# Down projection of a hybrid decoder step with seven products per pair of output tiles, and a new order around its compressed attention

## What is computed

```python
def conformer_conv(u, buf, w, b, ln_g, ln_b):          # width 31, each channel by itself
    xx = jnp.concatenate([buf, u], 1)
    y = dwconv_valid(xx, w) + b
    return jax.nn.silu(layer_norm(y, ln_g, ln_b)), xx[:, -(CONV_WIDTH - 1):]

def conv_ffn(h, buf, w_up, cw, cb, w_down):
    z = h @ w_up
    gate, up = z[..., :D_FF], z[..., D_FF:]
    gc = dwconv_valid(jnp.concatenate([buf, gate], 1), cw) + cb
    return (jax.nn.silu(gc) * up) @ w_down, ...
...
x = x + jnp.concatenate([o_nsa, c], -1) @ w_out
x = x + conv_ffn(rms_norm(x, ffn_g), ...)              # D_FF = 2816, D_MODEL = 1024
```

## Time and profile before

| | |
|---|---|
| median of 3 runs | 2145.61 us (2143.18 to 2148.26) |
| the profiled execution's own time | 2146.83 us |
| its span, first to last instruction | 2145.0 us |
| granted TensorE clock, mean | 0.959 of full |
| TensorE busy with matmuls | 2032.3 us, 95% |
| TensorE weight loads (beside them) | 1567.8 us, 73% |
| VectorE busy | 1154.1 us, 54% |
| ScalarE busy | 365.6 us, 17% |
| GpSimd busy | 113.5 us, 5% |
| DMA queues, share of 16 engines | 23.6% and 4.0% |
| chain that ended last | PE 90%, DVE 6%, ACT 3%, issue 1% |

### The profile page before, as it was taken

One profiled execution on the slowest core, in us unless ns is written; L12 is line 12 of the kernel. 1 busy time (PEld: TensorE's weight loads), 2 busy tenths in 40 slices (PEclk: granted clock), 3 DMA queues, 4 the chain that ended last, 5 costly groups with the idle time before them and its releaser, 6 DMA issues.

```text
span 2145.0 us, 26339 instructions
## 1 busy us (share of the span) xinstructions
PE 2032.3 (95%) x9926; PEld 1567.8 (73%) x9926; DVE 1154.1 (54%) x2762; ACT 365.6 (17%) x957; POOL 113.5 (5%) x219
## 2 busy tenths in 40 slices
PE   8999779999999999999999988799989999999999
PEld 5767656777777777777776677567767777777777
DVE  4997566554066666600069974755431767765000
ACT  1012156212110000100000121652221100000000
POOL 1002030000000000000000020300000000000000
PEclk9998679999999999999999986899999999999999
DMA  6203262652312222111231022226522122221112
...
DMA packets 109985, 200.23 MB, mean 93 GB/s; under 512 B 13698, under 2 KB 81555, under 8 KB 104611
## 3 DMA queue, kind: packets, MB, share of 16 engines
q1 hardware_dynamic: 103618, 167.01, 23.6%
...
## 4 chain that ended last, share of the span: by engine, by line
PE 90%; DVE 6%; ACT 3%; issue 1%; DMA 0%; POOL 0%; DVEq 0%
PE ps L908 26%; PE ps L536 18%; PE ps L689 9%; PE ps L549 9%; PE ps L579 8%; PE ps L977 2%; PE ps L861 2%; PE ps L735 2%; PE ps L521 2%; PE ps L807 1%; PE ps L766 1%; PE ps L674 1%; PE ps L595 1%; PE ps L752 1%; PE ps L618 1%
## 5 line engine op out<-in xcount | busy, mean ns | idle before, releaser
L536 PE MATMUL ps<-rC,rB 128*128 128x288 f32 x1056 | 257.1, 406 | 0.0
L536 PEld LDWEIGHTS ps<-rC,rB 128*128 128x128 f32 x1056 | 200.6, 190 | 55.4
L1395 DVE SCALAR_TENSOR_TENSOR catT<-XC,par,catT 128x512 f32<-128x512 f32 x240 | 180.4, 752 | 8.3
L1811 DVE TENSOR_TENSOR xT<-xT,ps 128x576 f32<-128x576 f32 x14 | 10.6, 754 | 289.2 <-PE ps L536 250.9
L908 PE MATMUL ps<-catT,rD 128*128 128x288 f32 x528 | 131.6, 406 | 0.0
L689 PE MATMUL ps<-WR,rD 128*128 128x254 f32 x512 | 120.7, 393 | 0.0
L908 PEld LDWEIGHTS ps<-catT,rD 128*128 128x128 f32 x528 | 100.3, 190 | 27.7
L908 PE MATMUL ps<-catT,XC 128*128 128x288 f32 x480 | 119.8, 406 | 0.4 <-DVE rD L1766 0.4
L908 PE MATMUL ps<-rA,WR 128*128 128x288 f32 x448 | 117.8, 406 | 0.0
L689 PEld LDWEIGHTS ps<-WR,rD 128*128 128x128 f32 x512 | 99.9, 197 | 16.6 <-issue 0.3
L908 PEld LDWEIGHTS ps<-catT,XC 128*128 128x128 f32 x480 | 91.0, 190 | 26.2 <-issue 1.2
...
## 6 DMA issues: line engine op xcount, KB each, us to landing
...
WR<-in_kvc SPq DMA_DIRECT2D x128, 128.0 KB
...
```

What stands on the lines that cost most here:

```text
L536: ins = mm(ps[:, bank + hf, 0:HN], w[:, k * P:(k + 1) * P], rhs[:, k, hf * HN:(hf + 1) * HN], start=k == 0, stop=k == K - 1)
L1395: stt(yc[:, 0:SEQ], xc[:, k:k + SEQ], w, yc[:, 0:SEQ], ALU.mult, ALU.add)
```

## The change

Four things.

**contract** makes the output tiles in four pairs q. The product of a pair of output tiles with the 22 tiles of `actT` is cut into 2 x 2 blocks both ways (two output tiles, two halves of 11 tiles (FH), left and right columns) and made with seven products of 11 `mm` each, p1 to p7, which stand for eight. Four of them read sums of weight blocks (DS1 to DS4, by `s1` to `s4`, for each pair) and four read sums of activations (DT1 to DT3, `b12` in place, DT4, by `t1` to `t4`, once a layer), all made by VectorE. VectorE adds each product to the quarters of `xT` that it belongs to, in one instruction with the bank broadcast. Two weight tiles now lie in all of `rB` (`DW[0]`), the next two in `rD` (`DW[1]`), and a pair's loads wait for the pair that had the place; the first load into `rD` also waits for the layer's `ff` output to be written. In the last pair of layer 0 the order is p1, p2, p7, p6, p4, p5, p3. As the second tile of pair 0 lies where ring slots 4 and 5 are, the last pair of expand, f = 21, goes to slots 0 and 1, which pair 19 holds. The next layer's w_qkv is loaded before its w_glu, and w_glu waits for DS1 to DS3, which lie in `WR`.

**taps** runs the taps over the prompt's tokens alone, with a `step` after each; the samples' convolution of a tile is one product of 64 x 31 elements, one sum over the 31 and one addition of the bias.

**compress**: all five `heads(t)` come ahead of `ln_var` and the reciprocal; ScalarE squares the heads of tiles 2 to 4 first (tile 4 into a place of its own in `rA`).

**compressed scores**: `keys_T` and `cmp_scores` run within `hidden(l, 1, 1)`, after 4 and 8 of its 16 `mm`; the sample's second products, the first two prompt scores and `cmp_turned` are interleaved at the start of `prompt`, and VectorE's and ScalarE's orders follow.

The diff, cut to its core (indentation shortened):

```diff
+        def up_slots(f):
+            return (0, 1) if f == FT - 1 else ((2 * f + 4) % 6, (2 * f + 5) % 6)
...
-        s = (n + 4) % 6
+        s = up_slots(n // 2)[n % 2]
         seen_of["unit_made"] += 1
         if n >= 2:
-            sp.wait_ge(sh["unit_made"], seen_of["unit_made"] - 6)
+            sp.wait_ge(sh["unit_made"], seen_of["unit_made"] - (6 if n // 2 < FT - 1 else 3 + n % 2))
...
+        if l:
+            for ch in range(2):
+                qkv(l, ch)
         for s in range(4):
+            if l and s % 2 == 0:
+                sp.wait_ge(sh["down_made"], 28 * l - (1 if s else 3))
             ring(s, I["w_glu"][l, s])
-        if l:
-            sp.wait_ge(*count("down_made", KD))
-        for ch in range(2):
-            qkv(l, ch)
-        if l:
-            sp.wait_ge(*count("ff_out", 16))
+        if l == 0:
+            for ch in range(2):
+                qkv(l, ch)
+        else:
+            sp.wait_ge(sh["down_made"], 28 * l)
         sp.dma_start(rD[:, 4096:8192], I["w1"][l]).then_inc(sh["w1_in"], 16)
...
-        sp.wait_ge(sh["unit_made"], seen_of["unit_made"])
+        sp.wait_ge(sh["unit_made"], seen_of["unit_made"] - 2)
         down(l, 1)
+        sp.wait_ge(*count("act_done", FT))
         if l + 1 < DEPTH:
-            sp.wait_ge(*count("act_done", FT))
             sp.dma_start(par[:, :], I["par"][l + 1]).then_inc(sh["par_in"], 16)
+        sp.wait_ge(*count("ff_out", 16))
         for m in range(2, KD):
-            sp.wait_ge(sh["down_made"], l * KD + m - 1)
+            if m >= 4 and m % 2 == 0:
+                sp.wait_ge(sh["down_made"], 28 * l + 7 * (m // 2 - 1))
             down(l, m)
+        sp.wait_ge(sh["down_made"], 28 * l + 21)
...
-        prompt_hidden(l, 1)
-        keys_T(NCS)
+        prompt_hidden(l, 1, lambda: keys_T(NCS))
         prompt_second(l, 0)
         hidden(l, 1, 0)
         prompt_second(l, 1)
-        keys_T(NCP)
-        cmp_scores(l)
-        hidden(l, 1, 1)
-        sample_second(l, 1, 0, CG[0])
-        sample_second(l, 1, 1, CG[0])
-        cmp_turned()
-        pe.wait_ge(sh["vct_kept"], NJOB * l + 3)
+        hidden(l, 1, 1, {3: lambda: keys_T(NCP), 7: lambda: cmp_scores(l)})
...
+        pe.wait_ge(*count("cs_max"))
         scores(0)
+        sample_second(l, 1, 0, CG[0])
+        sample_second(l, 1, 1, CG[0])
+        scores(1)
         keys_T(NCS)
-        scores(1)
+        cmp_turned()
         pe.wait_ge(sh["kct_kept"], NJOB * l + 3)
+        pe.wait_ge(sh["vct_kept"], NJOB * l + 3)
         pe.wait_ge(*count("ct_kept", 2))
...
+        def product(bank, w, h, each=None):
+            for k in range(FH):
+                if each:
+                    pe.wait_ge(*count(each))
+                ins = mm(ps[:, bank, 0:HN], w(k), h(k), start=k == 0, stop=k == FH - 1)
+            ins.then_inc(sh["down_made"], 1)
...
+            def p1():
+                after(ahead + 1)
+                product(0, lambda k: w[:, 0, k], lambda k: actT[:, k, left], None if q else "act_done")
+            def p2():
+                after(ahead + 5)
+                product(1, lambda k: w[:, 0, FH + k], lambda k: actT[:, FH + k, left], None if q else "act_done")
+            def p3():
+                after(ahead + 6, ds=4)
+                product(4, lambda k: DS4[k // 4][:, k % 4], lambda k: actT[:, FH + k, right])
+            def p4():
+                after(ahead + 7, dt=4)
+                product(5, lambda k: w[:, 1, FH + k], lambda k: DT4[k // 5][:, k % 5])
+            def p5():
+                after(ahead + 3, ds=1, dt=1)
+                product(2, lambda k: DS1[:, k], lambda k: DT1[:, k])
+            def p6():
+                after(own + 2 if q else 0, ds=3, dt=3)
+                product(1 if q else 6, lambda k: DS2[:, k], lambda k: actT[:, k, right])
+            def p7():
+                after(ahead + 4, ds=2, dt=2)
+                product(3, lambda k: DS3[k // 10][:, k % 10], lambda k: DT3[:, k])
...
+            p1()
+            if q and not last:
+                square_sum(2 * q - 2, 6, sq2, KD)
+            p2()
+            if q and not last:
+                square_sum(2 * q - 1, 6, sq2, KD)
+            if q < 3 or last:
+                p5()
+                p7()
+                p6()
+                p3()
+                p4()
+                count("x_upd", 2)
+            else:
+                p7()
+                p6()
+                p4()
+                p5()
+                half_sum(6, 6, 0, False)
+                half_sum(7, 6, 0, True)
+                p3()
+                pe.wait_ge(*count("x_left", 2))
                 pe.wait_ge(*count("x_upd"))
-            if m == 0:
-                for f in range(FT):
-                    pe.wait_ge(*count("act_done"))
-                    for hf in range(2):
-                        ins = mm(ps[:, hf, 0:HN], WD[:, 0, f * P:(f + 1) * P], actT[:, f, hf * HN:(hf + 1) * HN],
-                                 start=f == 0, stop=f == FT - 1)
-            else:
-                ins = unit(WD[:, m % 2], actT, 2 * (m % 2), FT)
-            ins.then_inc(sh["down_made"], 1)
-            if m and not last:
-                square_sum(m - 1, 6, sq2, KD)
+                half_sum(7, 6, 1, False)
+            if q == 0 and not last:
+                pe.wait_ge(sh["d_added"], 28 * l + 5)
...
+        head_squares(*TT[3])
+        head_squares(*TT[4])
...
+        turned_heads(2)
         root(lnrs)
-        head_squares(*TT[4])
-        turned_heads(2)
         tanhed(CG[0][0], NCS)
         turned_heads(3)
         tanhed(CG[0][1], NCS)
-        act.wait_ge(*count("qk_done", 2))
+        act.wait_ge(*count("qk_done", 3))
         turned_heads(4)
...
-                stt(yc[:, 0:SEQ], xc[:, k:k + SEQ], w, yc[:, 0:SEQ], ALU.mult, ALU.add)
-                ins = stt(ys, xs[:, :, k:k + DS], w, ys, ALU.mult, ALU.add)
-            if k < CW - 1:
-                step(ins)
+                ins = stt(yc[:, 0:SEQ], xc[:, k:k + SEQ], w, yc[:, 0:SEQ], ALU.mult, ALU.add)
+            step(ins)
         if last == CW:
-            ins.then_inc(sh["conv_made"], 1)
+            xs, ys = xc[:, XS0:XW], yc[:, SEQ:NT]
+            every = bass.AP(xs.tensor, xs.offset, [list(xs.ap[0]), [XSEG, DB], [1, DS], [1, CW]])
+            w = PV[:, 16 + 34 * c:16 + 34 * c + CW].unsqueeze(1).unsqueeze(1).to_broadcast([P, DB, DS, CW])
+            step(tt(TM.rearrange("p (b n k) -> p b n k", b=DB, n=DS), every, w, ALU.mult))
+            step(dve.tensor_reduce(ys, TM.rearrange("p (n k) -> p n k", k=CW), X, ALU.add))
+            ts(ys, ys, PV[:, 16 + 34 * c + CW:17 + 34 * c + CW], None, ALU.add).then_inc(sh["conv_made"], 1)
...
         head_means(1)
         heads(0)
+        heads(1)
+        head_means(2)
         ln_centre()
-        head_means(2)
-        heads(1)
-        ln_var()
         head_means(3)
         heads(2)
+        head_means(4)
+        heads(3)
+        heads(4)
+        ln_var()
+        dve.wait_ge(*count("posb_kept"))
+        gelu_in(0, NCS, 0)
         dve.wait_ge(*count("std_made"))
         step(dve.reciprocal(lnrs, lnrs))
-        head_means(4)
-        heads(3)
-        dve.wait_ge(*count("posb_kept"))
-        gelu_in(0, NCS, 0)
-        heads(4)
         gelu_in(1, NCS, 0)
...
         mask(0)
+        gelu_out(1, NCS, 0)
+        cmp_weight()
+        key_means(NCS)
+        mask(1)
+        weight(0)
         key_norm(NCS)
-        for v in range(16):
+        if l:
+            dve.wait_ge(sh["s_kept"], l * NPR)
+        dve.wait_ge(*count("tr_kept", 10))
+        for h in range(2):
+            hp = slice(HD * h, HD * (h + 1))
+            for g in range(G):
+                ins = dve.tensor_copy(QB[hp, :, 32 * h + 8 * g:32 * h + 8 * g + 8],
+                                      QT[hp, g, SEQ:NT].rearrange("p (b i) -> p b i", b=DB))
+        ins.then_inc(sh["qb_made"], 1)
+        for v in range(1, 16):
...
+        def t1():
+            tt(DT1, b12, b11, ALU.subtract).then_inc(sh["dt_made"], 1)
+        def t3():
+            tt(DT3, b22, b12, ALU.subtract).then_inc(sh["dt_made"], 1)
+        def t2():
+            dve.wait_ge(sh["dt_made"], 4 * l + 2)
+            tt(b12, b22, DT1, ALU.subtract).then_inc(sh["dt_made"], 1)
+        def t4():
+            dve.wait_ge(sh["dt_made"], 4 * l + 3)
+            for i, (a, b) in enumerate(((0, 5), (5, 10), (10, 11))):
+                ins = tt(DT4[i], b21[:, a:b], b12[:, a:b], ALU.subtract)
+            ins.then_inc(sh["dt_made"], 1)
+        def s1(q):
+            dve.wait_ge(*count("wb_in" if q % 2 else "wa_in", 32))
+            w = DW[q % 2]
+            tt(DS1, w[:, 1, 0:FH], w[:, 1, FH:FT], ALU.add).then_inc(sh["ds_made"], 1)
+        def s3(q):
+            w = DW[q % 2]
+            tt(DS3[0], w[:, 0, 0:10], w[:, 1, 0:10], ALU.subtract)
+            tt(DS3[1], w[:, 0, 10:FH], w[:, 1, 10:FH], ALU.subtract).then_inc(sh["ds_made"], 1)
+        def s2(q):
+            dve.wait_ge(sh["ds_made"], 16 * l + 4 * q + 2)
```

(65 more changed lines are left out.)

159 lines of the change are left out of this document (86 added, 73 removed).

## The result

The changed kernel takes 2075.97 us (median of 4 runs, 2074.83 to 2076.76) and the kernel before, run beside it on the same chip, 2144.69 (2143.18 to 2148.26): a ratio of 0.9677 with a 95% interval of 0.966 to 0.9694, so 68.7 us or 3.2% faster. The forecast was 2090 and 55.3 gained, with a range of 2077 to 2103. The profiled execution of the changed kernel took 2076.76 and its span is 2075.0, against 2146.8 and 2145.0 before: 70.1 less, 14.8 more than forecast on the same footing.

What follows compares the result with a forecast made beforehand. TensorE, busy 95% of the span, was taken as the bound. Contract 42.7, less expand 15.1, plus compress 19.6, scores 7.8 and the end 0.3 gave 55.3 us gained, median 2090, range 2077 to 2103.

Steps and rivals of the forecast that it cites:

- Contract: Contract, both layers: 308 `mm` a layer in place of 352, 42.7 us gained, VectorE's sums costed at nothing.
- Expand: Expand's last ring slot: pair 21 loads later, TensorE waits 5.85 a layer, plus 1.7 of clock; 15.1 lost together.
- one fall costs 1.6, and I add 1.7 a layer: Expand, after the new hole: TensorE's clock falls, 1.7 us a layer added, between ends of nothing and 3.
- Taps: Taps: a tile 1.4 us better, but glu(3) and `project` 1.3 late; the end of the taps 0.4 earlier.
- Compress: Compress: heads ahead of the norm let `prompt_T` begin 9.5 us earlier, 10.1 in layer 1; sum 19.6.
- Scores within the MLP: From L635 to the third scores: two holes filled, then VectorE bounds; 3.9 us gained a layer, 7.8 in both.
- Rival (b): Clock stays up in expand's hole and through `prompt_hidden` and the MLP after: 12.2 us, time 2078; chance 0.13.
- a clock above 0.97: Sign listed as showing the prediction wrong: TensorE's granted clock above 0.97.
- (a): Contract: VectorE's sums come late, p6 waits 6.2 us a layer, 12.4 in all, time 2103; chance 0.12.
- (c): Compress and prompt: waits only change names, root and reciprocal hold TensorE; 27.4 us gone, time 2118; chance 0.07.
- (d): Taps: samples' product may pay by the row, slower than before; 2165 us at 14 a tile; chance 0.02.
- (e): Expand: the ring change costs nothing, as loads come earlier than read; time 2075 us; chance 0.02.

Runs made afterwards that it cites:

- b1_fill_heads: Changed kernel with six extra products (12 records) in the hole ahead of `prompt_T`: 2065.06 us, ratio 0.9632.
- c4_all: Changed kernel with ring change undone, two contract waits later, VectorE's taps dealt otherwise, third scores ahead of the samples' turned keys: 2041.17 us, ratio 0.9532.
- c5_all_filled: c4_all with two extra products (4 records) ahead of the prompt's transposes: 2043.03 us, ratio 0.9535.

## Why the prediction was right or wrong

The direction and the parts were right, and the sum came out 14.8 low. The steps that failed are two terms of the clock: the stretch at contract's start was not taken away (3.4), and the records whose holes were filled were costed at the old clock (4.8). The rest is 3.5 in compress, 1.6 of queue in the scores' part, 2.0 of chance at the start, less 0.5 elsewhere.

**Contract.** Right in kind: 616 records, no wait for VectorE. The term was mis-sized, 43.0 with the end for 46.2, since the working called contract "a solid line, 88 records in 21.34 us", while the row above it in the earlier trace rows had 23.27 for the first tile. Those 1.9 were a stretch at the lower clock, present in both layers before and in neither after. The step that failed is "Expand ... one fall costs 1.6, and I add 1.7 a layer": I added a fall in the new hole and did not take away the one that stood at contract's start. The two experiments on the ring and the filled hole show that it is one stretch that moves. Without the stretch contract is 1.7 a layer shorter (176 records in 42.92 and not 44.60), so by the traces the hole costs 11.8 net (15.2 less 3.4) and not 15.1; the run of it alone gave 8.5, and 12.2 in the profiled execution.

**Expand.** The hole was forecast as 5 for the load and 1 for the sums, then 1.7 of clock. It is 5.2, no wait for the sums (8 records at the lower clock, 4.18, cover VectorE's 2.7), and 2.5 of clock: 7.7 and 7.5 against 7.55. The sum agreed, with two errors of a kind that cancel.

**Taps.** Right: glu(3) waits 3.5, and undoing the part changes nothing that can be measured.

**Compress.** The mechanism was right and the size off: 23.1 in the traces and 22.7 when undone, for 19.6. In layer 1 VectorE had waited 3.4 for the means and not 1.7 as in layer 0, and the walk, written out for layer 0, says only "The same walk through layer 1 gives 10.1". With that 1.7 it would have been 11.8, and at `prompt_T` the traces have 12.1 there, and 10.5 in layer 0 for 9.5.

**Scores within the MLP.** Here the step that failed is the largest: "scores 5.4, the last eight 4.4 (at the lower clock)", that is, the clock of the kernel before was carried over to records whose holes had been filled. They take 3.68 and 3.68. Of the 3.2 a layer that were missed this is 2.4, and putting the scores back ahead of the product costs 2.9 of clock a layer beside the 2.5 of hole. The hole of about 5 ahead of `keys_T` is 3.9.

**The start.** 2.0 of the surplus of the profiled run is no part of the change: the stretch at the lower clock within the first 30 us was 6.8 long in the profile of before and 3.4 in that of after, and it took either length, or none, in profiles of kernels that do not differ there.

**The rivals.** Rival (b), the clock stays up, came to 2078, near the measured 2076, and that nearness is luck. It named two places, and in both the clock fell as before: in expand's hole (8 records in 4.18), and through `prompt_hidden` (32 records in 7.09) into the MLP after it (8.72 before, 8.48 after in layer 0). Its 12.2 did not come there; what came is at contract's start, which it does not name, and at the scores and the last products of the MLP, of which it names at most the latter. Its price of 178 for the upper clock stands in no row: b1_fill_heads shows 118, and with that (b) would have been 2070. The mean granted clock, 0.959 before, is 0.969 to 0.971 in the four runs, at the edge of the sign "a clock above 0.97". The right thought in (b), that filled holes keep the clock up, was given 0.13 because of one row: TensorE busy for all 6 us and still at 0.50. That row was read as "small products alone do not lift the clock", and in c4_all the same product stands at 0.50 again. What I did not ask is whether they also lower it. In b1_fill_heads, in both layers, the same product ran at 1.00 all through. The Trainium skill (TensorE: Matmul & The Clock Gate, What's actually happening) has a throttled default that activity releases; here the trace agrees only in part, as the product of c4_all is busy for 7.09 of 7.09 us at 0.50.

(a) did not occur: no product waits for sums; moving contract 2.0 earlier makes the first wait 0.78, so the margin of p5 was 1.2, near the 1.3 forecast. (c), (d) and (e) are refuted: the waits did not keep their size, product and sum of the samples' part take 2.23 and 2.22 as forecast, and the ring change alone costs 8.5.

What stays open: why the extra records of b1_fill_heads kept the clock at 1.00. It is not the closed hole: in layer 1 a hole of 1.65 was left and the clock held, while c5_all_filled had none ahead of the transposes and lost it. The two kernels differ in the number of extra records, twelve and four, and no run separates their number from their time or from where they stand. What made taps and compress of layer 0 bring 11.1 and not 9.5 was not tried by itself either.
